# Modulation vectors of layers 1 to 3 on VectorE instead of TensorE, and a reordered last mLSTM step, in a four-layer decoder trunk

## The reference

```python
cond = jax.nn.silu(c)                                    # (B, 1024)
for layer in range(4):
    mod = cond @ ada_w[layer] + ada_b[layer]             # (B, 6*1024)
    sh1, sc1, g1, sh2, sc2, g2 = jnp.split(mod, 6, axis=-1)
    h = modulate(rms_norm(x, norm_mix_g[layer]), sh1, sc1)
    y = short_conv_mixer(h, ...) if layer % 2 == 0 else mlstm_mixer(h, ...)
    x = x + (1 + g1)[:, None, :] * y
    h = modulate(rms_norm(x, norm_ffn_g[layer]), sh2, sc2)
    x = x + (1 + g2)[:, None, :] * conv_ffn(h, ...)
```

## Time and profile before

| | us |
|---|---|
| median of 3 runs | 2952.39 (2951.89 to 2952.41) |
| the profiled execution's own time | 2951.92 |
| its span on the slowest core | 2950.3 |
| TensorE busy | 2849.4 (97%) |
| VectorE busy | 1989.7 (67%) |
| ScalarE busy | 1210.7 (41%) |
| GpSimd busy | 951.9 (32%) |
| share of the 16 DMA engines of the main weight queue | 60.2% |

### The profile page before, as it was taken

The page is one execution under the profiler, slowest core; times in us unless marked ns, Lnnn a source line. Parts: engine busy times, 40 slices in busy tenths (PEclk is TensorE's granted clock), DMA queues, the critical chain, the costliest instruction groups (busy, mean ns, idle before and its releaser), DMA issues.

```text
span 2950.3 us, 45095 instructions; the slowest of 8 cores (2939.3 to 2950.3 us)
## 1 busy us (share of the span) xinstructions
PE 2849.4 (97%) x15410; PEld 1358.4 (46%) x15696; DVE 1989.7 (67%) x2679; ACT 1210.7 (41%) x1910; POOL 951.9 (32%) x861
## 2 busy tenths in 40 slices
PE   3999999999999999999999999999999999999998
PEld 1444444444454544444444444444445454444443
DVE  1767676787565667678766767668766565766873
ACT  3323452453444345335322335425535352542551
POOL 1110352353252434316311014405405262441440
PEclk9999999999999999999999999999999999999999
DMA  9887678677834357667675548576671616457533
GB/s 178 141 110 103 96 101 110 98 107 101 115 45 72 58 86 115 93 104 108 101 96 71 83 70 121 83 111 103 101 105 30 101 25 95 75 78 108 80 58 114
DMA packets 290800, 276.48 MB, mean 94 GB/s; under 512 B 9616, under 2 KB 284304, under 8 KB 290576
## 3 DMA queue, kind: packets, MB, share of 16 engines
q0 software_dynamic: 283232, 256.00, 60.2%
q1 hardware_dynamic: 7344, 17.58, 1.9%
HBM read 521.15 MB, written 8.39 MB: 179 GB/s over the span
## 4 chain that ended last, share of the span: by engine, by line
PE 93%; DMA 2%; DVE 1%; issue 1%; ACT 1%; POOL 0%; DVEq 0%; SPq 0%; ACTq 0%; POOLq 0%
PE ps L228 93%; DMA ring<-ada_w 1%; ACT work L188 1%; DMA x_sb<-xT 1%; PE ps L237 1%; DVE work L191 1%; DMA ring<-ml_w_in 0%; DVE x_sb L201 0%; DVE work L201 0%; SPq L242 0%; DVEq L261 0%; POOL work L215 0%; POOL ring L242 0%; POOL work L194 0%; ACT L188 0%
## 5 line engine op out<-in xcount | busy, mean ns | idle before, releaser
L228 PE MATMUL ps<-h_sb,ring 128*128 128x512 bf16 x8000 | 1776.0, 380 | 22.0 <-ACT h_sb L188 8.0
L228 PEld LDWEIGHTS ps<-h_sb,ring 128*128 128x128 bf16 x8192 | 795.1, 98 | 959.3 <-issue 19.8
L201 DVE SCALAR_TENSOR_TENSOR work<-ps,params_sb,work 128x1023 bf16<-128x1023 f32 x704 | 901.9, 1281 | 279.1 <-ACT halo_u L188 160.6
L228 PE MATMUL ps<-work,ring 128*128 128x512 bf16 x3637 | 807.3, 379 | 12.3 <-DVE work L191 4.6
L188 ACT ACTIVATE work<-ps,params_sb 128x1024 bf16<-128x1024 f32 x352 | 423.5, 1203 | 702.1 <-PE ps L228 702.0
L194 POOL TENSOR_TENSOR work<-work 128x1024 bf16<-128x1024 bf16 (+2 forms) x288 | 511.9, 1791 | 391.0 <-ACT work L188 360.7
L201 DVE SCALAR_TENSOR_TENSOR x_sb<-ps,mods,x_sb 128x512 f32<-128x512 f32 x480 | 359.1, 750 | 359.3 <-PE ps L228 349.0
L228 PEld LDWEIGHTS ps<-work,ring 128*128 128x128 bf16 x3712 | 361.4, 98 | 440.8 <-issue 9.6
L188 ACT ACTIVATE h_sb<-work,mods 128x512 bf16<-128x512 f32 x192 | 138.1, 722 | 417.6 <-DVE work L201 401.1
L188 ACT ACTIVATE work<-ps 128x512 bf16<-128x512 f32 (+3 forms) x352 | 178.5, 520 | 231.4 <-PE ps L228 220.3
L188 ACT ACTIVATE work<-work 128x1024 bf16<-128x1024 bf16 (+4 forms) x224 | 211.3, 943 | 110.3 <-DVE work L191 90.8
(11 more groups left out here) (67 smaller groups left out, 1107.8 us busy)
## 6 DMA issues: line engine op xcount, KB each, us to landing
ring<-ffn_w_up POOLq DMA_DIRECT2D x80, 1024.0 KB, 12.0
ring<-ada_w POOLq DMA_DIRECT2D x48, 1024.0 KB, 10.9
ring<-ffn_w_down POOLq DMA_DIRECT2D x30, 1024.0 KB, 10.1
ring<-ml_w_in POOLq DMA_DIRECT2D x24, 1024.0 KB, 9.4
ring<-sc_w_in POOLq DMA_DIRECT2D x32, 512.0 KB, 9.3
ring<-ffn_w_down POOLq DMA_DIRECT2D x16, 768.0 KB, 8.9
ring<-sc_w_in POOLq DMA_DIRECT2D x8, 1024.0 KB, 11.1
ring<-sc_w_out POOLq DMA_DIRECT2D x8, 1024.0 KB, 9.4
```

Of the source, the lines that this page charges most:

```text
L201: return self.op("dve", lambda e: e.scalar_tensor_tensor(out=out, in0=in0, scalar=scalar, in1=in1, op0=op0, op1=op1), reads, [out])
L228: return self.op("pe", lambda e: e.matmul(out, lhsT=lhsT, rhs=rhs, start=start, stop=stop), [lhsT, rhs], [out], mark=mark)
```

## The change

Four things are changed.

1. The modulation blocks of layers 1 to 3, except the two late ones of layer 1, are computed by VectorE. A second copy of the weights, `ada_t`, holds the outputs as rows. A block of it is 512 outputs, as 4 groups (m) of 128 partitions by 1024. VectorE multiplies a group with `cond_b`, silu(c) repeated on all partitions, and its accumulator sums the row into one element of `mods` per partition: one `scalar_tensor_tensor` of 128x1024 in bf16 for 128 outputs, which writes the products back over the weights in the slot.
2. These instructions are not emitted at the spot. They go into a list, `ada_q`, and `ada_tick` takes one after each group of the following block in the up part and after every second group in the down part. The block's `done_block` comes with its fourth instruction. While the list is not empty, `use_block` is called with `hold=1`.
3. `cond_b` takes the place of the accumulator `acc_v` in `work`, and `acc_v` becomes the second half of `rs_v`. One transfer (`c_rows`, 512 KB) and one ScalarE instruction make `cond_b`.
4. In the last mLSTM chunk `step_t(3)` is emitted before `step_num(7)` instead of after `step_p(7, 0)`, and the transposes of chunks 4 to 7 take the bank that was used longest ago.

```diff
-        acc_v = cv_([512], F32)
+        acc_v = rs_v[:, 1, :]
         ssum_v = cv_([2, 512], BF16)
+        cond_b = cv_([D], BF16)
...
+        c_tmp = view(work, 45056, [D], F32)
+        S.dma("sp", c_tmp, dr["c_rows"], crow_sem)
...
-            if isinstance(src, tuple):
+            if kc < 0:
+                dst = ring[:, s, :, :].rearrange("p k n -> p (k n)").rearrange("p (m k) -> p m k", m=4)
+                S.dma("pool", dst, src, ring_sem[s], writes=[ring[:, s, :, :]])
+            elif isinstance(src, tuple):
...
+        def wblock_rows(w_ap, r0):
+            src = w_ap[r0:r0 + 512, :].rearrange("(m p) k -> p m k", p=128)
+            blocks.append((src, -1, 1024))
+            return len(blocks) - 1
...
-            def reg(j):
+            on_dve = li > 0
+
+            def reg(j, pe=False):
+                if on_dve and not pe:
+                    return wblock_rows(dr["ada_t"][li], j * 512)
                 return wblock(dr["ada_w"][li], 0, D, j * 512, 512)
+
+            def consume_dve(j, bi):
+                slot = use_block(bi).rearrange("p k n -> p (k n)").rearrange("p (m k) -> p m k", m=4)
+
+                def one(m):
+                    q = 4 * j + m
+                    S.stt_acc(slot[:, m, :], slot[:, m, :], cond_b, mods[:, slot_l, q:q + 1])
+                    if m == 3:
+                        done_block(bi)
+                return [lambda m=m: one(m) for m in range(4)]
...
+            ada_q = []
+
+            def ada_tick():
+                if ada_q:
+                    ada_q.pop(0)()
...
                 a, aj, abi = extra
-                a[1](aj, abi)
                 if a is ada0:
+                    a[1](aj, abi)
                     if aj == 11:
                         a[2](40, 48)
-                elif li == 0:
+                    return
+                while ada_q:
+                    ada_q.pop(0)()
+                ada_q.extend(a[3](aj, abi))
...
                 for (kind, i, ncols, bi), extra in seq[:nup]:
-                    slot = use_block(bi)
+                    slot = use_block(bi, hold=1 if ada_q else 0)
...
                             S.tt(acc[:, 0:2], acc[:, 0:2], corr_u[:, q, :], ALU.add)
+                        ada_tick()
...
                             if t2 == 1:
                                 side.tick_b()
+                            else:
+                                ada_tick()
...
                 def step_t(c, bank=1):
-                    pt = ps[:, bank, :].bitcast(BF16)
+                    pt = (next_bank() if bank is None else ps[:, bank, :]).bitcast(BF16)
...
                         o_group()
+                        step_t(3)
                     step_num(c)
                     post_a(c)
                     if c > 0:
                         o_group()
                     step_p(c, 0)
-                    if c >= 4:
+                    if 4 <= c < 7:
                         step_t(c - 4)
...
-                hooks = [(lambda c=c: step_t(c, (0, 1, 2, 3)[c - 4])) for c in range(4, 8)]
+                hooks = [(lambda c=c: step_t(c, None)) for c in range(4, 8)]
```

More of the change, by code:

```diff
@@ L277, in build_program @@
     dr["ada_w"] = nc.dram_tensor("ada_w", [nl, D, 6 * D], F32, kind="ExternalInput").ap()
+    dr["ada_t"] = nc.dram_tensor("ada_t", [nl, 6 * D, D], F32, kind="ExternalInput").ap()
+    dr["c_rows"] = nc.dram_tensor("c_rows", [128, D], F32, kind="ExternalInput").ap()
     dr["ffn_w_up"] = nc.dram_tensor("ffn_w_up", [nl, D, 2 * DFF], F32, kind="ExternalInput").ap()
@@ L391, in build_program @@
         st_sem = S.dma_sem("st")
+        crow_sem = S.dma_sem("crow")
         S.dma("sp", params[:, :], dr["params"], misc_sem)
@@ L485, in consume, with finalize @@
                 done_block(bi)
-            def finalize(lo, hi):
+            def finalize(lo, hi, pe=not on_dve):
                 md = mods[:, slot_l, lo:hi]
-                S.tt(md, psa[:, lo:hi], params[:, pb + P_ADAB + lo:pb + P_ADAB + hi], ALU.add)
+                S.tt(md, psa[:, lo:hi] if pe else md, params[:, pb + P_ADAB + lo:pb + P_ADAB + hi], ALU.add)
                 for (o_sc, o_g, pg) in ((8, 16, P_NMG), (32, 40, P_NFG)):
@@ L496, in finalize @@
                         S.ts(a_g, a_g, 1.0, None, ALU.add)
-            return reg, consume, finalize
+            return reg, consume, finalize, consume_dve
         ada0 = ada_parts(0)
@@ L767, in ada_step @@
                 a, aj, abi = extra
-                a[1](aj, abi)
                 if a is ada0:
+                    a[1](aj, abi)
                     if aj == 11:
                         a[2](40, 48)
-                elif li == 0:
+                    return
+                while ada_q:
+                    ada_q.pop(0)()
+                ada_q.extend(a[3](aj, abi))
+                if li == 0:
                     if aj in (3, 9):
-                        a[2](*((0, 16) if aj == 3 else (16, 40)))
+                        ada_q.append(lambda: a[2](*((0, 16) if aj == 3 else (16, 40))))
                 elif aj in (5, 11):
-                    a[2](24 * (aj // 6), 24 * (aj // 6) + 24)
+                    ada_q.append(lambda: a[2](24 * (aj // 6), 24 * (aj // 6) + 24))
             def run():
                 early = []
+                if li == 0 and hf == 0:
+                    S.act(cond_b, c_tmp, AF.Silu)
                 if tail:
@@ L888, in mlstm_phase @@
             if late:
-                b_late.append(late[0](10))
+                b_late.append(late[0](10, True))
             b_k = wblock(w_in, 0, D, 512, 512)
             if late:
-                b_late.append(late[0](11))
+                b_late.append(late[0](11, True))
             b_v = [wblock(w_in, 0, D, 1024 + 512 * i, 512) for i in range(2)]
@@ L946, in run @@
                     late[1](11, b_late[1])
-                    late[2](40, 48)
+                    late[2](40, 48, True)
                 v_slot = [use_block(b_v[0]), use_block(b_v[1], hold=1)]
@@ L1178, in _launch @@
         "ada_w": np.ascontiguousarray(inp["ada_w"][l0:l1]),
+        "ada_t": np.ascontiguousarray(np.asarray(inp["ada_w"][l0:l1]).transpose(0, 2, 1)),
         "ffn_w_up": np.ascontiguousarray(inp["ffn_w_up"][l0:l1]),
@@ L1192, in _launch @@
         m["params"] = params_list[b]
+        m["c_rows"] = np.ascontiguousarray(np.broadcast_to(np.asarray(inp["c"][b], np.float32)[None, :], (128, D)))
         in_maps.append(m)
```

## The result

The changed kernel takes 3004.7 to 3006.1 us (three executions), against 2951.9 to 2952.4 before: a ratio of 1.018 [1.016, 1.020], some 53 us slower. Forecast were 3061 and a range of 2993 to 3100: direction, place and mechanism are as forecast, the loss is half as large.

The account below looks back on a forecast made before the run. TensorE, holding 93% of the chain that ended last, was taken as the bound. From 2951.9: -27.2 - 6.8 + 101.6 + 27.2 + 5.7 + 8.4 = +108.9, 3060.8, forecast as 3061 us, range 2993 to 3100.

Parts of the forecast that it names:

- TensorE without 34 blocks: FFN of layers 1 to 3: 34 modulation blocks leave TensorE at 0.80 us each, gain 27.2 us.
- mLSTM: Output projection's bank waits go, cover between state updates is lost: net 1.7 us in each of four halves, gain 6.8 us.
- 16 refill waits: FFN up part, after g0, g1, g2: TensorE waits 5.9 us 7 times, 6.7 us 9 times, 101.6 us lost.
- clock behind them: After each of the 16 up-part waits the granted clock falls to 0.50: 1.7 us each, 27.2 us lost.
- VectorE at the fourth spot: FFN up part: VectorE lags about 1.4 us in hf 1, half a microsecond in hf 0; 5.7 us for six phases.
- down part: FFN down part, behind the fifth spot: the refill comes 1.4 us late, six times, 8.4 us lost.
- start (`ada_w`, `h_sb`): Load of `c_rows` and the silu before the FFN's first group: nothing; with that cover gone, about 1 us each.
- the landing: Up-part refill, first of two transfers issued together: lands 11.7 us after issue; range ends took 9.9 and 12.9.
- Half 0's first accumulation: FFN up part, hf 0: the first accumulation waits for GpSimd's product until 8.35 us after the block's start.
- layer 3's FFN: Sign: layer 3's FFN, without modulation blocks, should take the same time as before.
- VectorE alone: Rival: transfers land in time, VectorE bounds hf 1 with period 30.7 against 27.6 us; 2954 us, chance 0.06.
- The cover holds: Rival: accumulations disappear in VectorE's 33% idle time and the slot is refilled in time; 2918 us, chance 0.06.

Follow-up runs that it names:

- 15 blocks: Changed kernel, but VectorE keeps only blocks behind g3 in half 0 and two per down part; of the mLSTM part only the banks: 2928.6 to 2932.6 us, 0.993.
- alone: Kernel before with only the mLSTM part of the change (part 4): 2941.3 to 2944.8 us, 0.996 of the kernel before.
- the repeat: The changed kernel unaltered, run once more on the same chip as the other experiments: 2996.9 and 3000.6 us, 1.014 of the kernel before.
- two kernels: Changed kernel with accumulations on a row outside the ring, 2956.0 to 2960.1 us; and with two accumulations behind each up-part group, 2959.9 to 2962.6 us.
- the kernel without the slot reads: Changed kernel whose accumulations read and write a row of ones outside the ring, the slot free at once: 2956.0 to 2960.1 us, 1.002 of the kernel before.

## Why the forecast was right in kind and too large

The difference of the two profiled spans is 3003.1 - 2950.3 = 52.8 us. By the forecast's steps:

| step | forecast | found |
|---|---|---|
| TensorE without 34 blocks | -27.2 | -27.2 (taken; 15 blocks gave 11 of 12) |
| mLSTM | -6.8 | -6.9 (waits); -7.9 alone |
| 16 refill waits | +101.6 | +61.3 |
| clock behind them | +27.2 | +22.9 |
| VectorE at the fourth spot | +5.7 | 0 |
| VectorE behind the first spot of half 1 | 0 | +1.1 |
| down part | +8.4 | 0 |
| start (`ada_w`, `h_sb`) | 0 | +2.9 |
| `ml_w_in` (3.3 to 1.1) and `sig` (0.6 to 0) | 0 | -2.8 |
| sum | +108.9 | +51.3, within 1.5 of 52.8 |

**The failed step is the size of the refill wait**, the landing in it above all. Number, place and chain are as written: 7 in half 0, 9 in half 1, none at the fourth spot. But a wait is 3.8 us instead of 5.9 and 6.7. On core 7 the first transfer of a pair landed 8.8 to 11.7 us after its issue, in the mean of the 16 10.1, where I took 11.7: 1.6 us by 16 is 26 of the 40 us too much. The other 14 are in the earlier issue (21.0 instead of 21.6 in half 0), in the period of the two blocks (27.8, not 27.6) and in the start after the landing (0.1, not 0.2). Inside the earlier issue one term was too small: from the end of the fourth accumulation to the issue are 0.55 us (1166.42 to 1166.97), not 0.1. The accumulation costs 1.14 us between starts (1157.76 to 1158.90) and not 1.36; the read of the accumulator, 0.08, begins with the next instruction and costs nothing of its own. The bounds for it, 1.29 to 1.51, were both too high: the nearest row was a `scalar_tensor_tensor` that does not accumulate, at its own 1.28, and it was no lower bound. That the accumulating form is two instructions, as the Trainium skill says ("VectorE: DVE Perf Modes", section "Two Vector instructions with no wait between them"), the trace confirms with its row of `DVE_READ_ACCUMULATOR`.

Why was 11.7 too long? I had read landings on the slowest core alone, core 4. The first of two transfers at the same spot of the kernel before, on two neighbouring cores (a group each; the last line is the landing of the two, min, median, max):

```profile
L242 POOL DMA_DIRECT2D ring<-ada_w x1: 953/953/953, 1095.1 to 1095.1; - x1
...
DMA to landing us min/median/max: 8.2/10.3/12.5
```

That was core 7. The same for core 0:

```profile
L242 POOL DMA_DIRECT2D ring<-ada_w x1: 953/953/953, 1099.1 to 1099.1; - x1
...
DMA to landing us min/median/max: 10.9/13.5/16.1
```

**Half 0's first accumulation** waited for GpSimd's product as forecast: 1.61 us instead of 1.22 (1153.64, product 1152.06 to 1154.17).

**The clock** is about right per wait and wrong in the count. TensorE's 128 matmuls take 27.79 us at full clock (1145.98 in the timeline above, after a wait of 2.35). After 4.83 us:

```profile
597.85 30.11 PE L228 MATMUL ps<-h_sb,ring 128*128 128x512 bf16 x128 [4.83 <-DMA ring<-ffn_w_up]
630.30 9.87 PE L228 MATMUL ps<-h_sb,ring 128*128 128x512 bf16 x45 [2.34 <-DMA ring<-ffn_w_up]
```

2.32 us more, and the stretches (busy time per engine, then the granted clock, the share of DMA, GB/s) show why:

```profile
597.90:601.30 3.40, 3.40 (x9) 1.17 (x10) 1.72 (x2) 0.00 (x0) 3.40 (x3) 0.50 1.21 198
...
630.30:633.00 2.70, 2.70 (x13) 1.26 (x14) 2.60 (x4) 1.95 (x3) 2.62 (x3) 1.00 1.16 154
1176.20:1179.40 3.20, 3.20 (x8) 1.15 (x9) 1.71 (x2) 0.50 (x1) 3.20 (x3) 0.50 1.23 205
```

The granted clock stood at 0.50, 1.2 GHz, after the waits of 4.83 and of 2.42, and at 1.00 after that of 2.34. Of the 16 blocks 12 show an excess, 1.4 to 2.7 us each and 22.9 in all. The length of the wait alone doesn't decide: on core 7 waits of 3.30 and 3.65 us left the clock at 1.00 and waits of 3.38 and 3.45 did not, and on core 1 a wait of 2.02 was followed by 0.50 (timeline, then the stretch):

```profile
1143.98 29.47 PE L228 MATMUL ps<-h_sb,ring 128*128 128x512 bf16 x128 [2.02 <-DMA ring<-ffn_w_up]
1144.20:1147.60 3.40, 3.40 (x10) 1.20 (x9) 1.90 (x2) 0.69 (x2) 3.40 (x3) 0.50 1.15 170
```

What else decides is open.

**The down part** lost nothing: in the one phase looked at, the transfer behind the fifth spot landed 8.9 us after its issue, and 11.7 was again in my sum. **The fourth spot** lost nothing instead of 5.7. The 1.1 us of waits for L191 are six of 0.18 each, two behind the first spot of every half 1 (585.60 and 589.40 in layer 0). That the cheaper accumulation and the time that VectorE gains behind each late refill explain this is argued, not shown. **The start** I had put at nothing; the 2.9 us lie in the waits for `ada_w` (16.8 to 17.7) and `h_sb` (34.9 to 36.9), of which the second differs by more between runs of one kernel (26.4 in the repeat), so I don't read them as the change's. Of the other signs, **layer 3's FFN** takes as long as before, 479.1 us from its first up matmul to the end against 478.5.

Of the rivals, the one that decided next was VectorE alone: with the refill out of the way two kernels stand at 2956 to 2963, where it said 2954. That the number fits is partly luck: it had 36 us of VectorE's lag and no clock, and with the refill in time the waits were 21.5 us, followed by a slow clock. "The cover holds" was never near: every core shows 15 or 16 of the waits.

## What to carry to other kernels

Before work goes to an engine that is "a third idle", follow the buffer that the work holds. Here 5 us of accumulations, spread over four groups, kept a ring slot for 21 us of a 28 us period, and the refill behind it had 7 us left for a flight of 9 to 12. Move such work to the spots where the next use of its buffer is far: that version was faster than both kernels. Doing it sooner took the refill waits away and put waits for VectorE in their place, and gained nothing over the kernel before. Look for the second bound behind the first, and read transfer times on several cores, not on the slowest alone.

## What the runs showed of the hardware

- `scalar_tensor_tensor` of 128x1024 bf16 with an accumulator took 1.22 us and 1.14 between starts; the same without accumulator 1.28. The accumulator's read took 0.08 and overlapped the next instruction.
- At one and the same place of the program a 1 MB block (2 MB read) landed after 8.0 us on one core and 11.0 on another.
- Waits of TensorE of 2.34, 3.30 and 3.65 us left the granted clock at 1.00 in the changed kernel; waits of 2.02 (core 1) and 2.42 (core 7) were followed by 0.50 for about 3.2 to 3.4 us. In the kernel without the slot reads, waits of 2.0 to 2.1 us were followed by 1.7 us of loss each.
